# A hybrid attention / PEER layer on one core: two more ring slots for gathered rows, laid in the last eighth of the query weights

## The chip, the cores and the metric

One core of a Trainium2 chip runs the whole kernel. The metric is the device time of one execution in microseconds (us), as the median of several runs. TensorE is called PE, VectorE DVE, ScalarE ACT, GpSimd POOL and SyncE SP, as in the profile.

## What is computed

One layer over 1024 latent tokens of width 1024, with 256 context tokens. The token mixer is attention plus a bidirectional recurrence; its output goes through `w_out`, a norm and a residual. Then comes the part in which most of the time lies, product-key retrieval of single-neuron experts. The reference for it, per chunk of 128 tokens:

```python
q = (xc @ wq).reshape(PEER_CHUNK, PEER_HEADS, 2, PEER_DKEY // 2)
s = jnp.einsum('nhpd,hpkd->nhpk', q, subkeys).astype(jnp.float32)
s1, i1 = lax.top_k(s[:, :, 0], PEER_TOPK)
s2, i2 = lax.top_k(s[:, :, 1], PEER_TOPK)
...
top_s, pos = lax.top_k(cand_s, PEER_TOPK)
idx = jnp.take_along_axis(cand_i, pos, axis=-1)
g = jax.nn.softmax(top_s, axis=-1).astype(xc.dtype)
act = jax.nn.gelu(jnp.einsum('nhkd,nd->nhk', u[idx], xc))
return jnp.einsum('nhk,nhkd->nd', g * act, v[idx])
```

So each token picks 8 x 16 = 128 experts out of 16384, and for each of them a row of 1024 float32 of `u` and one of `v` are read.

## The kernel before

**Chunks.** The latent tokens are eight chunks of 128 (`NX = 8`). A chunk n passes through attention, a post part (output projection `out`, norms, the query projection `q(0)` to `q(3)` with `wq`, its transposes `turn_keyed`, the comparison with the subkeys `compare`), and a routing part on DVE that gives the indices of its 128 experts per token. Then its u rows and v rows are gathered. The work on the experts of chunk n runs beside the attention and post of chunk n+1.

**Gathers.** A "slot" is one indirect DMA of POOL (L619, in `gather`): one row of u or v for each of the 128 tokens, 4 KB to each of 128 partitions, 512 KB in all. A chunk has 128 u slots and 128 v slots, the kernel 2048 gathers. A u slot is consumed on DVE (L1565, `u_slots`), a product with `hx_cur` summed over the row. A v slot is consumed on PE (L2100, `v_slots`): two matmuls of 512 columns (four records in the profile) with a column of weights that ACT makes (L960, `SELS = 8` of them ahead).

**The ring.** Gathers land in `RING = 11` buffers of 4 KB a partition. The order of the gathers is fixed by a number for each, its place (`u_place`, `v_place`), and place p uses buffer p modulo 11. The order: chunk 0's 128 u slots; then per chunk 60 v slots (`LEAD`), which stand alone, then sixteen runs of twelve, 8 u slots of the next chunk and 4 v slots of this one, then 4 v slots (`TAIL`). The last chunk ends with its 68 v slots alone. Before a gather, `freed` lets POOL wait until the user of the place 11 back has counted up `u_used` (DVE) or `v_used` (PE). The user waits in `landed` for the buffer's own semaphore `got[r]`.

**PE's order** is written out by hand: `fill` puts v slots between the pieces of attention and post. In the post part of chunk n these are, in order: `out`, the transposes of the normed tokens, `q(0)`, `q(1)`, `q(2)`, `turn_keyed(0)`, `q(3)`, `compare(0)`, `turn_keyed(1)`, `compare(1)`. Each `q(i)` is eight matmuls over the slices kt = 0 to 7 of `wq`, 512 columns each (two records each in the profile, L2034). After routing, the indices are turned on PE (L2090) behind the lead's v slots, and DVE copies them out (L1589, in `turn_indices`); only then may the next chunk's v gathers start. DVE's L1401 is the maximum over the attention scores.

**SP's queue** is in program order: per chunk it loads `lc` (the recurrence's output, `load_l`, L495), the next `qz` (`load_qz`, L500), stores the finished chunk (L517) and loads a piece of x (`load_x`, L511). `wq` is loaded once, in two pieces; its last slice, `wq[:, KT - 1, :]`, is 8 KB a partition (L489).

**Memory.** A buffer `arena` holds most things. At its end lie `pr`, `pT`, `qc`, `lc` and `att`, the buffers of attention; `lc` and `att` (512 floats each) are dead from the end of the output projection of a chunk until the next `lc` is loaded.

## Time and profile before

| | |
|---|---|
| runs | 3435.26, 3441.04, 3443.61 us |
| median | 3441.04 us |
| span of the profiled execution (its only time) | 3447.3 us |
| mean granted clock of PE, share of full | 0.782 |
| busy PE / DVE / POOL / ACT | 2466.8 / 2047.0 / 2087.7 / 785.3 us |
| DMA | 1163.76 MB, mean 338 GB/s, of it 1084.36 MB from POOL's queue |
| gathers on POOL | 2048, 960.0 + 977.6 us busy |

The span runs from the first to the last instruction. Busy time counts neither waits nor the issue of DMAs by SP. "Idle before, released by" tells what event ended an engine's wait; where the name is "remote", the profile could not tie it to an instruction. The first eighth or so of the span is start-up and the recurrence; from 374 us on gathers run without end. One chunk takes some 372 us.

### The profile page before, as it was taken

What the parts mean: (1) busy time and instruction counts of PE and PEld (TensorE: products, weight loads), DVE (VectorE), ACT (ScalarE), POOL (GpSimd) and SP (SyncE); (2) the same over time, 40 slices, a digit from 0 to 9 for tenths busy, and PEclk for the clock granted to TensorE, in tenths of its full rate; (3) what the DMA queues carried; (4) which work ended last, traced back from release to release, by engine and by line L of the source; (5) the groups of instructions that cost most, each with busy time, mean ns of one, the idle gap of its engine ahead of it and who ended that gap; (6) DMA issues with size and microseconds to landing.
All of it is one profiled execution on the core that took longest, in us unless ns stands there. A gap on an engine that the chain in (4) does not pass through costs nothing.

```text
span 3447.3 us, 29321 instructions
## 1 busy us (share of the span) xinstructions
PE 2466.8 (72%) x9222; PEld 1078.6 (31%) x9222; DVE 2047.0 (59%) x4621; ACT 785.3 (23%) x1888; POOL 2087.7 (61%) x2167
## 2 busy tenths in 40 slices
PE   7978977768676776677777867787767766533476
PEld 4844654324221432134222422143213422000011
DVE  4785786666655666656656566665665666565300
ACT  2265111122112221222122221222122212100121
POOL 6910254566666666666666666666666666666665
PEclk8989987886789667865797578956796688855699
DMA  8533499799999999999999999999999999999998
GB/s 319 179 140 113 142 337 358 288 358 362 349 371 367 360 364 367 362 368 358 364 367 375 361 364 372 372 358 366 364 361 370 361 355 359 372 379 368 364 367 323
DMA packets 335937, 1163.76 MB, mean 338 GB/s; under 512 B 40485, under 2 KB 51365, under 8 KB 333608
## 3 DMA queue, kind: packets, MB, share of 16 engines
q0 software_dynamic: 297792, 1084.36, 83.6%
q1 hardware_dynamic: 37994, 77.54, 6.3%
q8 instruction: 76, 1.25, 0.1%
q14 instruction: 75, 0.61, 0.0%
HBM read 1148.13 MB, written 13.63 MB: 337 GB/s over the span
## 4 chain that ended last, share of the span: by engine, by line
PE 29%; POOL 16%; issue 14%; another core or an unknown queue 13%; DMA 12%; DVE 11%; ACT 4%; SPq 1%; DVEq 0%; ACTq 0%; POOLq 0%
POOL arena L619 16%; DMA arena<-in_v,arena 9%; PE psum L2100 9%; DVE arena L1565 6%; PE psum L1931 4%; PE psum L1899 4%; DMA arena<-in_u,idx_u 2%; PE psum L2034 2%; PE psum L1920 2%; PE psum L1946 2%; PE psum L1781 1%; PE psum L1956 1%; PE psum L1980 1%; ACT arena L883 1%
## 5 line engine op out<-in xcount | busy, mean ns | idle before, releaser
L1565 DVE CUSTOM_DVE_ANT_0 arena<-arena,psum 128x1024 f32<-128x1024 f32 x1024 | 1215.6, 1218 | 413.3 <-DMA arena<-in_u,idx_u 379.4
L619 POOL DMA_INDIRECT arena<-in_u,idx_u x1024 | 960.0, 937 | 652.8 <-issue 267.8
L2100 PE MATMUL psum<-arena 128*32 128x512 f32 x4096 | 1013.0, 744 | 445.6 <-DMA arena<-in_v,arena 305.4
L619 POOL DMA_INDIRECT arena<-in_v,arena x1024 | 977.6, 955 | 522.1 <-issue 256.8
L2100 PEld LDWEIGHTS psum<-arena 128*32 128x32 f32 x4096 | 181.8, 124 | 1185.3 <-issue 1036.6
L960 ACT ACTIVATE arena<-arena 128x32 f32<-128x32 f32 x1024 | 277.6, 314 | 1166.4 <-PE psum L2100 580.1
L1899 PE MATMUL psum<-kT,arena 64*128 64x512 f32 (+1 forms) x384 | 252.4, 810 | 56.2 <-issue 26.9
L1920 PE MATMUL psum<-ident,arena 128*128 128x128 f32 x560 | 137.5, 378 | 174.5 <-issue 110.3
L1401 DVE TENSOR_REDUCE small<-psum 128x1 f32<-128x1280 f32 x64 | 95.4, 1491 | 278.4 <-remote 220.8
L1931 PE MATMUL psum<-v,arena 128*128 128x64 f32 x1120 | 230.4, 395 | 27.3 <-ACT arena L883 24.0
L2034 PE MATMUL psum<-wbig,arena 128*128 128x512 f32 x512 | 242.4, 628 | 4.5 <-issue 3.4
L1931 PEld LDWEIGHTS psum<-v,arena 128*128 128x128 f32 x1120 | 221.4, 304 | 45.4 <-ACT arena L883 38.5
L883 ACT ACTIVATE arena<-psum 128x512 f32<-128x512 f32 x168 | 87.9, 523 | 403.6 <-remote 287.1
L1920 PEld LDWEIGHTS psum<-ident,arena 128*128 128x128 f32 x560 | 82.7, 186 | 296.6 <-issue 196.6
L1899 PEld LDWEIGHTS psum<-kT,arena 64*128 64x128 f32 x384 | 100.7, 279 | 185.7 <-issue 147.7
L2034 PEld LDWEIGHTS psum<-wbig,arena 128*128 128x128 f32 x512 | 100.7, 202 | 142.1 <-issue 140.3
L1426 DVE TENSOR_SCALAR small<-small 128x1 f32<-128x1 f32 x24 | 3.6, 152 | 225.8 <-ACT arena L977 164.4
L1964 PE MATMUL psum<-rows,ident 1*128 1x512 f32 x128 | 60.2, 824 | 77.9 <-issue 42.7
L1980 PE MATMUL psum<-arena 128*128 128x512 f32 x224 | 115.0, 668 | 0.0
L826 ACT ACTIVATE arena<-psum,small 128x64 f32<-128x64 f32 x64 | 20.0, 313 | 309.0 <-remote 197.5
L819 ACT ACTIVATE arena<-psum,small 128x1280 f32<-128x1280 f32 x64 | 84.8, 1325 | 23.6 <-issue 13.2
L1565 DVE DVE_READ_ACCUMULATOR2_ANT arena<- 128x1 f32 x1024 | 84.6, 83 | 0.0
(268 smaller groups left out, 2154.9 us busy)
## 6 DMA issues: line engine op xcount, KB each, us to landing
arena<-in_u,idx_u POOLq DMA_INDIRECT x1024
arena<-in_v,arena POOLq DMA_INDIRECT x1024
arena<-in_w_mod POOLq DMA_DIRECT2D x20, 512.0 KB, 4.3
wbig<-in_wq SPq DMA_DIRECT2D x1, 7168.0 KB, 19.7
arena<-in_w_mod SPq DMA_DIRECT2D x12, 512.0 KB, 4.1
arena<-in_xin SPq DMA_DIRECT2D x5, 1024.0 KB, 9.6
arena<-in_w_mod SPq DMA_DIRECT2D x2, 2048.0 KB, 10.7
wbig<-in_w_mod SPq DMA_DIRECT2D x2, 2048.0 KB, 20.5
```

The costliest lines, as they stand in the source:

```text
L619: pool.indirect_dma_start(ring[:, r, :], None, t[table], bass.IndirectOffsetOnAxis(idx[:, j:j + 1], 0)).then_inc(got[r], 16)
L819: A(pr, psum[:, score_at(n):score_at(n) + KEYS], ACT.Exp, scale=HD ** -0.5, bias=small[:, a:a + 1], accum_out=small[:, b:b + 1]).then_inc( ...
L883: A(pT[:, 4 * g:4 * g + k, :], bank(3)[:, 0:k * P], ACT.Copy).then_inc(S["pt_out"], 1)
L960: A(sel[:, j % SELS, :], hot[:, QP - 1 - i:2 * QP - 1 - i], ACT.Copy, scale=wT[:, n:n + 1])\
L1401: ch.link(V.tensor_reduce(small[:, a:a + 1], psum[:, score_at(n):score_at(n) + KEYS], AX, ALU.max))
L1565: V.tensor_tensor_reduce(ring[:, r, :], ring[:, r, :], hx_cur, 1.0, 0.0, ALU.mult, ALU.add, act_[:, j:j + 1]).then_inc(S["u_used"], 1)
L1899: ins = M(psum[:, at_ + b:at_ + b + w], lhsT=qc[o:o + 64, h // 2, :], rhs=kT[o:o + 64, b:b + w], start=True, stop=True)
L1920: ins = T(bank(3)[:, j * P:(j + 1) * P], pr[:, kt * P:(kt + 1) * P], ident[:, :])
L1931: ins = M(pv, lhsT=pT[:, kt, :], rhs=v[:, kt, 64 * (h % 2):64 * (h % 2) + 64], start=(kt == 0), stop=(kt == NTOK - 1))
L1980: return M(bank(i), lhsT=att[:, kt, :] if kt < 4 else lc[:, kt - 4, :], rhs=wo[:, kt, 512 * i:512 * i + 512], start=(kt == 4), stop=(kt == 3))
L2034: ins = M(bank(i), lhsT=hxT[:, kt, :], rhs=wq[:, kt, 512 * i:512 * i + 512], start=(kt == 0), stop=(kt == KT - 1))
L2100: ins = M(bank(4 + b)[QP * g:QP * g + QP, :], lhsT=sel[:, j % SELS, :], rhs=ring[:, r, 512 * b:512 * b + 512], start=(i == 0), stop=(i == ...
```

## The change

The ring gets 13 buffers. Eleven lie where they lay. Two lie over the last slice of the query weights, `wq[:, 7, 0:1024]` and `wq[:, 7, 1024:2048]`; `tile(r)` picks the place. Chunk 0 still uses that slice as it is, and POOL waits for `q_ready` 4 before the first gather into it. For chunks 1 to 7 the slice is loaded anew, in two halves of 512 KB, into the 1024 floats of `lc` and `att` (`wq_last`). The first half goes out when the output projection is done (`out_half`), and PE waits for it at the last slice of q(0); q(0) and q(1) use it. The second goes out when q(0) and q(1) are done (`q_ready` 4n+2), and PE waits for it at the last slice of q(2). The load of `lc` for the next chunk now waits until all four q are done. In `freed` and `landed` nothing is edited, but with `RING` 13 every wait names the user of 13 places back. To make room for semaphores some of the start-up are merged (`hot_made` into `filled`, `tanh_c` and `lam_exp`, `modT_ready` and `mod_rows`); this changes no order. Line numbers move: L619 is L637, L1565 is L1585, L2034 is L2059, L2100 is L2124, L2042 is L2066, L495 is L501, L500 is L515, L511 is L526, L517 is L532, L1589 is L1609.

```diff
@@ -54,7 +54,7 @@
 PAIRS = FULL + (TOPK - WIDE) * NARROW
 SLOTS = PH * TOPK
 HALF_SLOTS = SLOTS // 2
-RING = 11
+RING, ARENA_SLOTS = 13, 11
 QUADS, QP = 4, 32
 SELS = 8
 LABEL = 2 * NK
...
@@ -223,10 +223,12 @@
         qc = view(4 * P, 4, P)
         lc = view(4 * P, 4, P)
         att = view(4 * P, 4, P)
+        LC_AT = ATT_AT + 2 * KEYS + 4 * P
+        wq_last = arena[:, LC_AT:LC_AT + D]
 
         at[0] = 0
         wo = view(KT * D, KT, D)
-        ring = view(RING * D, RING, D)
+        ring = view(ARENA_SLOTS * D, ARENA_SLOTS, D)
         xm_new, xm_next, xm_cur = (view(D) for _ in range(3))
         qz = view(QZ_ROW)
         hx_new = qz[:, 0:D]
...
@@ -322,6 +324,10 @@
 
             return (c * STRIDE + place) % RING
 
+        def tile(r):
+
+            return ring[:, r, :] if r < ARENA_SLOTS else wq[:, KT - 1, (r - ARENA_SLOTS) * D:(r - ARENA_SLOTS + 1) * D]
+
         h_scr = nc.dram_tensor("h_scr", (NX, P, KT * P), F32, kind="Internal").ap()
         qz_scr = nc.dram_tensor("qz_scr", (NX, P, QZ_ROW), F32, kind="Internal").ap()
         l_scr = nc.dram_tensor("l_scr", (LF, P, SEQ), F32, kind="Internal").ap()
...
@@ -491,8 +497,17 @@
 
             def load_l(n):
 
-                sp.wait_ge(S["out_half"], 2 * n)
+                wait(sp, "q_ready" if n > 1 else "out_half", 4 * n if n > 1 else 2)
                 sp.dma_start(lc, l_scr[:, :, n * P:n * P + P].rearrange("f p c -> p f c")).then_inc(S["l_loaded"], 16)
+
+            def load_wq_last(n):
+
+                for half in range(2):
+                    if half:
+                        sp.wait_ge(S["q_ready"], 4 * n + 2)
+                    else:
+                        sp.wait_ge(S["out_half"], 2 * n + 2)
+                    sp.dma_start(wq_last, wqv[:, KT - 1, D * half:D * half + D]).then_inc(S["wq_last_loaded"], 16)
 
             def load_qz(n):
 
...
@@ -549,14 +564,17 @@
             sp.wait_ge(S["q_half_stored"], 16 * (NX - 2))
             sp.wait_ge(S["z_half_stored"], 16 * (NX - 2))
             load_x(1)
+            load_wq_last(1)
             load_l(2)
             load_qz(2)
             load_x(2)
             for k in range(NX - 3):
+                load_wq_last(k + 2)
                 load_l(k + 3)
                 load_qz(k + 3)
                 store(k)
                 load_x(k + 3)
+            load_wq_last(NX - 1)
             for c in range(NX - 3, NX):
                 store(c)
             sp.wait_ge(S["out_stored"], 16 * NX)
...
@@ -613,10 +631,10 @@
             for i in range(2):
                 pool.wait_ge(S["lru_stored%d" % i], 16 * LF // 2)
             ch.link(nc.gpsimd.memset(hot, 0.0))
-            nc.gpsimd.memset(hot[:, QP - 1:QP], 1.0).then_inc(S["hot_made"], 1)
+            nc.gpsimd.memset(hot[:, QP - 1:QP], 1.0).then_inc(S["filled"], 1)
 
             def gather(table, idx, j, r):
-                pool.indirect_dma_start(ring[:, r, :], None, t[table],
+                pool.indirect_dma_start(tile(r), None, t[table],
                                         bass.IndirectOffsetOnAxis(idx[:, j:j + 1], 0)).then_inc(got[r], 16)
 
             def u_gather(c, j):
...
@@ -624,6 +642,8 @@
                 if j % HALF_SLOTS == 0:
                     pool.wait_ge(S["idx_ready"], 2 * c + j // HALF_SLOTS + 1)
                     pool.sem_inc(S["passed"], 1)
+                if c == 0 and j == ARENA_SLOTS:
+                    pool.wait_ge(S["q_ready"], 4)
                 freed(c, u_place(c, j))
                 gather("u", idx_u, j, slot(c, u_place(c, j)))
 
...
@@ -1562,7 +1582,7 @@
 
                 for j in range(lo, hi):
                     r = landed(dve, c, u_place(c, j))
-                    V.tensor_tensor_reduce(ring[:, r, :], ring[:, r, :], hx_cur, 1.0, 0.0, ALU.mult, ALU.add,
+                    V.tensor_tensor_reduce(tile(r), tile(r), hx_cur, 1.0, 0.0, ALU.mult, ALU.add,
                                            act_[:, j:j + 1]).then_inc(S["u_used"], 1)
 
             def weights(c):
...
@@ -2031,8 +2051,12 @@
                             turn_first(i - 1)
                         if n == 0 and i and kt == 4:
                             compare_first(i - 1)
-                        ins = M(bank(i), lhsT=hxT[:, kt, :], rhs=wq[:, kt, 512 * i:512 * i + 512],
-                                start=(kt == 0), stop=(kt == KT - 1))
+                        w = wq[:, kt, 512 * i:512 * i + 512]
+                        if n and kt == KT - 1:
+                            if i % 2 == 0:
+                                pe.wait_ge(S["wq_last_loaded"], 16 * (2 * n - 1 + i // 2))
+                            w = wq_last[:, 512 * (i % 2):512 * (i % 2) + 512]
+                        ins = M(bank(i), lhsT=hxT[:, kt, :], rhs=w, start=(kt == 0), stop=(kt == KT - 1))
                     ins.then_inc(S["q_ready"], 1)
 
                 def turn_keyed(u):
...
@@ -2098,7 +2122,7 @@
                     for b in range(2):
                         g = (q + 2 * b) % QUADS
                         ins = M(bank(4 + b)[QP * g:QP * g + QP, :], lhsT=sel[:, j % SELS, :],
-                                rhs=ring[:, r, 512 * b:512 * b + 512], start=(i == 0), stop=(i == QP - 1))
+                                rhs=tile(r)[:, 512 * b:512 * b + 512], start=(i == 0), stop=(i == QP - 1))
                     ins.then_inc(S["v_used"], 1)
 
             def none(b):
```

SP's queue in the loop over the chunks; `in_wq` is the weights' tensor, `arena` the place of `wq_last`, `lc`, `qz` and x. Before:

```order
87 L495 DMA arena<-l_scr 128x4x128 [waits out_half]
88 L500 DMA arena<-qz_scr 128x1152 [waits hx_moved]
89 L511 DMA arena<-in_xin 128x1024 [waits xm_moved]
90 L495 DMA arena<-l_scr 128x4x128 [waits out_half]
91 L500 DMA arena<-qz_scr 128x1152 [waits hx_moved]
92 L517 DMA out<-arena 128x1024 [waits out_ready]
```

Now:

```order
87 L510 DMA arena<-in_wq 128x1024 [waits out_half]
88 L510 DMA arena<-in_wq 128x1024 [waits q_ready]
89 L501 DMA arena<-l_scr 128x4x128 [waits q_ready]
90 L515 DMA arena<-qz_scr 128x1152 [waits hx_moved]
91 L526 DMA arena<-in_xin 128x1024 [waits xm_moved]
92 L510 DMA arena<-in_wq 128x1024 [waits out_half]
93 L510 DMA arena<-in_wq 128x1024 [waits q_ready]
94 L501 DMA arena<-l_scr 128x4x128 [waits q_ready]
95 L515 DMA arena<-qz_scr 128x1152 [waits hx_moved]
```

Two loads stand ahead of the load of `lc` in each chunk, which waits for `q_ready` in place of `out_half`.

PE in the post part of a chunk, from the first matmul of q(0) to `turn_keyed(0)`; the rows left out are v slots. Before:

```order
1211 L2034 MATMUL psum<-wbig,arena 128x512 [waits wq_loaded,hxT_out]
1212 L2034 MATMUL psum<-wbig,arena 128x512 x10
...
1221 L2034 MATMUL psum<-wbig,arena 128x512 x11
...
1230 L2034 MATMUL psum<-wbig,arena 128x512 x2
1231 L2042 MATMUL psum<-ident,arena 128x128 [waits q_out]
1232 L2042 MATMUL psum<-ident,arena 128x128 x7
```

Now (`psum<-arena` on L2059 is a matmul with `wq_last`):

```order
1223 L2059 MATMUL psum<-wbig,arena 128x512 [waits wq_loaded,hxT_out]
1224 L2059 MATMUL psum<-wbig,arena 128x512 x6
1225 L2059 MATMUL psum<-arena 128x512 [waits wq_last_loaded]
1226 L2059 MATMUL psum<-wbig,arena 128x512 x3
...
1235 L2059 MATMUL psum<-wbig,arena 128x512 x4
1236 L2059 MATMUL psum<-arena 128x512
1237 L2059 MATMUL psum<-wbig,arena 128x512 x6
...
1246 L2059 MATMUL psum<-wbig,arena 128x512
1247 L2059 MATMUL psum<-arena 128x512 [waits wq_last_loaded]
1248 L2066 MATMUL psum<-ident,arena 128x128 [waits q_out]
1249 L2066 MATMUL psum<-ident,arena 128x128 x7
```

The order of matmuls is as before. The eighth matmul of each q reads `arena`, and the one of q(0) and of q(2) waits for a load.

## Rows read from the trace of the kernel before

**Rows 1.** The page: busy time (share) of the engines; the DMA in 40 slices.

```profile
PE 2466.8 (72%) x9222; PEld 1078.6 (31%) x9222; DVE 2047.0 (59%) x4621; ACT 785.3 (23%) x1888; POOL 2087.7 (61%) x2167
...
DMA  8533499799999999999999999999999999999998
```

**Rows 2.** Waits of POOL, whole kernel: total us, times, longest.

```profile
POOL arena L619 <- PE psum L2100: 259.6, 171, 20.1
POOL arena L619 <- remote: 187.2, 82, 4.9
POOL arena L619 <- DVE arena L1565: 148.5, 116, 23.1
```

**Rows 3.** Stretches: an attention, a lead, without a stall, after one, last v slots.

```profile
core 0: us, PE busy (x) PEld busy (x) DVE busy (x) ACT busy (x) POOL busy (x), PEclk, DMA share, GB/s
1119.00:1236.00 117.00, 93.15 (x340) 49.83 (x340) 73.62 (x130) 25.93 (x64) 75.62 (x81) 0.62 0.97 361
1384.00:1490.00 106.00, 73.15 (x296) 17.24 (x295) 61.23 (x258) 28.87 (x85) 68.49 (x72) 0.90 0.98 373
3010.00:3034.00 24.00, 5.99 (x18) 0.87 (x16) 17.99 (x29) 1.28 (x4) 16.27 (x18) 0.63 1.02 418
3036.00:3046.00 10.00, 6.80 (x16) 0.65 (x12) 1.46 (x3) 1.61 (x5) 7.50 (x8) 0.50 0.78 258
3262.00:3434.00 172.00, 129.81 (x500) 23.06 (x492) 3.52 (x5) 36.13 (x124) 110.54 (x117) 0.97 0.97 364
```

**Rows 4.** Timeline of PE and POOL, 3020 to 3037 (idle before, released by).

```profile
3020.83 5.67 PE L2100 MATMUL psum<-arena 128*32 128x512 f32 x16 [10.50 <-DMA arena<-in_v,arena]
...
3029.28 0.94 POOL L619 DMA_INDIRECT arena<-in_v,arena  x1 [0.30 <-issue]
...
3035.80 2.30 PE L2100 MATMUL psum<-arena 128*32 128x512 f32 x6 [9.31 <-DMA arena<-in_v,arena]
...
3036.26 0.94 POOL L619 DMA_INDIRECT arena<-in_v,arena  x1 [4.80 <-remote]
```

**Rows 5.** Waits of DVE in the attention 1119 to 1236.

```profile
DVE small L1401 <- remote: 40.2, 6, 8.1
```

**Rows 6.** Line 1589 (turned indices copied, DVE): its waits, us and times.

```profile
  remote: 58.6, 4
  PE psum L2090: 12.4, 3
```

**Rows 7.** Waits of POOL in 1384:1490, in 2990:3262, in 3262:3434.

```profile
POOL arena L619 <- PE psum L2100: 17.3, 14, 2.6
...
POOL arena L619 <- remote: 32.4, 9, 4.8
...
POOL arena L619 <- PE psum L2100: 33.8, 34, 3.6
```

**Rows 8.** Waits of POOL in the post 1236 to 1384.

```profile
POOL arena L619 <- remote: 21.2, 7, 4.9
```

**Rows 9.** DMA view of 1090 to 1110: SP's queue, packets, MB, share.

```profile
q1 hardware_dynamic: 288, 1.05, 14.0%
```

**Rows 10.** Timeline of SP, PE and DVE in a post and the lead behind it.

```profile
1287.33 0.37 SPq L495 DMA_DIRECT2D arena<-l_scr  x1
...
1318.58 9.71 PE L2034 MATMUL psum<-wbig,arena 128*128 128x512 f32 x22
...
1339.78 11.13 PE L2034 MATMUL psum<-wbig,arena 128*128 128x512 f32 x21 [1.09 <-issue]
...
1352.69 1.98 PE L2034 MATMUL psum<-wbig,arena 128*128 128x512 f32 x4
...
1473.25 0.69 DVE L1289 SCALAR_TENSOR_TENSOR arena<-arena 128x512 f32<-128x512 f32 x1
```

**Rows 11.** The page: DMA issues, KB each, us to landing.

```profile
arena<-in_w_mod SPq DMA_DIRECT2D x12, 512.0 KB, 4.1
...
wbig<-in_wq SPq DMA_DIRECT2D x1, 1024.0 KB, 8.2
```

More of the change, by code:

```diff
@@ L331, in layer @@
             "gains_loaded", "wm_loaded0", "wm_loaded1", "wm_loaded2", "wm_loaded3", "wm_used",
-            "acc_loaded", "staged_in0", "staged_in1", "mod_summed", "mod_rows", "mod_out",
-            "silu_ready", "tanh_c", "g1_ready", "a2_ready", "b2_ready", "g2_ready",
-            "modT_ready", "kvl_loaded", "x_loaded", "x_sq",
+            "acc_loaded", "staged_in0", "staged_in1", "mod_summed", "mod_turned", "mod_out",
+            "silu_ready", "c_tanh_lam_exp", "g1_ready", "a2_ready", "b2_ready", "g2_ready",
+            "kvl_loaded", "x_loaded", "x_sq",
             "x_var", "x_sd", "xn_ready", "xT_first", "xT_ready", "hT_vec", "hT_act", "kv_ready", "lru_ready",
@@ L691, in _ @@
             act.wait_ge(S["c_loaded"], 48)
-            A(csil, ccol, ACT.Tanh, scale=0.5).then_inc(S["tanh_c"], 1)
+            A(csil, ccol, ACT.Tanh, scale=0.5).then_inc(S["c_tanh_lam_exp"], 1)
             def x_norm(m):
@@ L801, in _ @@
             act.wait_ge(S["lam_ready"], 1)
-            A(lt[:, 1, :], lt[:, 0, :], ACT.Exp, scale=-1.0).then_inc(S["lam_exp"], 1)
+            A(lt[:, 1, :], lt[:, 0, :], ACT.Exp, scale=-1.0).then_inc(S["c_tanh_lam_exp"], 1)
             for m in range(1, NTOK // 2 - 1):
@@ L1085, in _ @@
             post(1, none)
-            act.wait_ge(S["hot_made"], 1)
+            act.wait_ge(S["filled"], 7)
             gelu(0)
@@ L1117, in _ @@
             V = nc.vector
-            dve.wait_ge(S["tanh_c"], 1)
+            dve.wait_ge(S["c_tanh_lam_exp"], 1)
             dve.wait_ge(S["filled"], 2)
@@ L1311, in _ @@
             V.tensor_copy(rowm, bank(4)).then_inc(S["mod_cols"], 1)
-            dve.wait_ge(S["modT_ready"], 1)
+            dve.wait_ge(S["mod_turned"], 1)
             dve.wait_ge(S["acc_loaded"], 32)
@@ L1615, in _ @@
             negmax(0, 0)
-            dve.wait_ge(S["mod_rows"], 1)
+            dve.wait_ge(S["mod_turned"], 2)
             dve.wait_ge(S["gains_loaded"], 48)
@@ L1729, in mod_sum @@
                                 start=True, stop=True)
-                ins.then_inc(S["mod_rows"], 1)
+                ins.then_inc(S["mod_turned"], 1)
             def keys(m, tt):
@@ L1835, in _ @@
                 ins = T(bank(6)[:, j * P:(j + 1) * P], rowm[:, j * P:(j + 1) * P], ident[:, :])
-            ins.then_inc(S["modT_ready"], 1)
+            ins.then_inc(S["mod_turned"], 1)
             pe.wait_ge(S["kvl_loaded"], 16)
```

8 lines of the change are left out of this document (4 added, 4 removed).

## Prediction

> **What bounds the kernel now.** I read the page first. Over the whole span no engine is full: PE is busy 72%, POOL 61%, DVE 59%, while the DMA line is at nine tenths or more from the ninth slice on [rows 1]. The loop is 2048 gathers. One takes 0.94 us of POOL and 0.30 of "issue" ahead of the next [rows 4], so back to back one leaves every 1.24 us, and 2048 of them are 2540 us of the span. What makes it longer stands in POOL's waits: 259.6 us for PE's v slots, 187.2 "remote", 148.5 for DVE's u slots [rows 2]. These are waits for a ring slot, and the change is aimed at them.
>
> Whether POOL or the memory sets the pace is told by the table of stretches [rows 3]. In an attention and in a lead the DMA engines show a share of 0.97 and 0.98 at 361 and 373 GB/s. But from 3010 to 3034, when POOL issues without a stall, they move 418 GB/s at 1.02, and just after a stall 258 at 0.78. The share hardly tells these states apart, the rate does: 418 GB/s is a gather of 0.524 MB each 1.25 us, POOL's own pace. So I hold the gathers to be limited by POOL and its stalls, not by the memory.
>
> How a stall arises is seen late in the kernel [rows 4]. POOL issues a v gather at 3029.28 and one more, then waits 4.80 us until 3036.26. The slot that it needs is that of eleven places before, whose matmuls by the records lie in the block 3020.83 + 5.67 = 3026.50. It is let go only when PE begins its next slots at 3035.80, and these wait for the gather of 3029.28 to land, 6.5 us after its issue. So the loop is: issue, landing, PE's next start, report, 7.0 us in all, and eleven slots let POOL issue two gathers in it. The Trainium skill (TensorE: Matmul & The Clock Gate, Part 3) has matmuls ending strictly in order, so that one increment on the last one is sound, and counts tens of ns for increments; here the report stands over 9 us behind the modelled end. By the page's figure there would be no stall to win here, and 11 us of the sum below would go.
>
> **The change, part by part.**
>
> *Two slots more.* The need of each gather moves two gathers back, 2 x 1.24 = 2.48 us. The stall of 4.80 becomes 2.3; one of up to 2.5 goes. What that is worth differs by stage.
>
> Attention: 81 gathers in 117 us, 1.44 each. DVE waits 40.2 us there for scores [rows 5], and PE, busy 93 of 117 at a clock of 0.62 [rows 3], sets the pace; POOL's stalls are its slack. I take **0** for the attention of every chunk.
>
> Lead: DVE has its routing done and then waits for the turned indices (L1589), which stand behind the 60 v slots on PE: 58.6 + 12.4 = 71.0 us in seven chunks, 10.1 each [rows 6]. POOL stalls for slots there 17.3 us, at most 2.6 at a time [rows 7], so two more slots could take nearly all. The bounds are 0 and -71, since behind that DVE's own routing is next. PE's late reports and the landings stay, so I take half: **-35**.
>
> Post: seven stalls, 21.2 us, the longest 4.9 [rows 8]. At most 7 x 2.48 = 17.4 goes. The stalls follow on each other, and where one is shortened POOL sooner stands before the next, as PE's q and turns take as long as before; I take -7, in the six chunks that have both tables in flight: **-42**, bounds 0 and -104.
>
> Part without attention (2990 to 3262): nine stalls, 32.4 us, longest 4.8 [rows 7]. At most 9 x 2.48 = 22. For the same reason half: **-11**.
>
> Last v slots (3262 to 3434): 33.8 us in 34 stalls [rows 7], 117 gathers in 172 us, where 117 x 1.24 = 145 [rows 3]. Bounds 0 and -27; PE is busy 130 of the 172 there and its slots follow each landing, so a quarter of the stalls: **-9**.
>
> *Fourteen loads of 512 KB.* Each chunk but the first loads 1.05 MB more, the bytes of two gathers. The nearest row is the stretch 1090 to 1110, where a store and a load of together 1.05 MB took 14.0% of 20 us: 2.8 us of all the engines [rows 9]. If POOL's pace and not the memory is the limit, some of it hides; I count all, 7 x 2.8 = **+20**. Bounds 0 and 20.
>
> *PE's new waits.* The first half is released by what now releases `lc`, at 1287.33, and q(0) reaches its last slice at 1318.58 + 14/22 x 9.71 = 1324.8 [rows 10]: 37 us for a load. The second half is released by q(1). Of the block at 1339.78 nine of 21 records belong to q(1): it ends at 1344.6. q(2) needs the half at its last matmul, at 1352.69 + 0.99 = 1353.7 [rows 10]. That is 9.1 us. Loads of 512 KB took 4.1 us on SP, one of 1024 KB took 8.2 [rows 11]; amid gathers I expect 6 to 8. Bounds 0 and, if q(1)'s report came 9.5 us late as in rows 4, 8.2 + 9.5 - 9.1 = 8.6. Between q(1)'s end and the need PE runs nearly without a break, unlike in rows 4, so I take 1 us in each chunk: **+7**. Behind that wait stand q(2)'s turns, q(3) and v slots on PE; ACT's and DVE's copies of q would be late, and the comparison.
>
> *Moved and merged.* SP's load of `lc` now stands behind both loads and behind q(3), so is issued some 75 us later than 1287.33. DVE reads it at 1473.25 [rows 10]: 256 KB have over 100 us. The load of `qz` behind it waits for DVE's copy anyway. POOL's new wait for `q_ready` 4 at the twelfth gather of chunk 0 is met before that chunk has indices. The merged semaphores belong to the start-up and keep its order. All at 0, covered by these times; if `lc` came late, DVE's mixing and the next `out` would be.
>
> **Sum.** -35 - 42 - 11 - 9 + 20 + 7 = -70. The profiled execution has a span of 3447.3, which is 6.3 above the median 3441.04. 3447.3 - 70 = 3377, less 6.3: **3371 us**, chance 0.50. A measurement can tell 0.3% (10 us) from no change.
>
> **Rivals.** (1) The memory is the limit, not POOL. For it: a share of 0.97 in every stage, with gaps in POOL's issue too short to empty the queues. Against it: 418 GB/s in rows 3. Then a slot more only makes gathers queue longer, and the loads' 7.34 MB are paid in full: at 361 GB/s 20 us, 3441 + 20 = **3461**, slower. It decides wherever the transfers in flight already keep the engines fed. Chance 0.17. The Trainium skill (DMA: Bandwidth & Descriptors, Specifications) gives a limit of about 358 GB/s of HBM for a core. By that rule the loop is at its ceiling and this rival is the outcome, with 7.34 MB / 358 GB/s = 20.5 us; the 418 GB/s kept up for 24 us speak against it.
> (2) q(1)'s report is late, and PE waits 8.6 us in seven chunks where I took 1: 3371 + 53 = **3424**, hardly faster; with a post that gains half as much, 3445. For it rows 4, against it that PE doesn't pause at that place. Chance 0.12.
> (3) The slots don't do what they say: PE reports only when it begins its next slots, so the stalls gather again two places later, and what is left pays for the loads: **3441**. Chance 0.08.
> (4) Every bound is reached: -71 - 104 - 22 - 27 + 20 = -204, or **3237**; half way from my sum to it, 3304. For it: POOL's stalls are 595 us in all [rows 2]. Chance 0.13.
>
> **Range.** 3300 to 3464: it leaves out the far half of (4) and what runs worse than (1). Faster by over 0.3%: 0.50 + 0.13 + 0.03 of (2) = 0.66. Slower: (1) and 0.01 of other mishaps = 0.18. The same: the rest, 0.16.
>
> **What would show it.** Right: in the part without attention the stalls of 4.8 us are about 2.3; the wait at L1589 (now L1609) falls to a half; a post is some 3 us shorter and an attention still 117; PE waits under 2 us at the last slice of q(2). Wrong: fewer stalls of POOL with the same GB/s and longer landings (rival 1), or several us on the `in_wq` loads (rival 2).

## The result, and the profile after

The changed kernel takes 3465.11 us in the median of 12 runs (3451.24 to 3478.39), the kernel before beside it 3442.19 (12 runs, 3431.53 to 3453.91). The ratio is 1.0065, with a 95% interval of 1.0046 to 1.0084: slower by 23 us, where 3371 was forecast. It lies one microsecond above the range. The profiled execution has a span of 3462.5 us, 15.2 above that of before.

The page of the changed kernel, with the rows that answer to [rows 1]:

```profile
PE 2409.3 (70%) x9222; PEld 1080.9 (31%) x9222; DVE 2039.2 (59%) x4621; ACT 784.2 (23%) x1888; POOL 2084.6 (60%) x2167
...
DMA  8533499699999999999999999999999998999998
```

At this level nothing seems to have happened: POOL is as busy, the DMA line as full. POOL's waits, to be held against [rows 2] (the waits for a slot in `wbig` are listed apart):

```profile
POOL arena L637 <- PE psum L2124: 227.8, 120, 11.3
POOL arena L637 <- remote: 169.7, 74, 5.6
...
POOL arena L637 <- DVE arena L1585: 109.4, 80, 24.6
...
POOL wbig L637 <- PE psum L2124: 46.9, 17, 26.9
POOL wbig L637 <- remote: 27.9, 11, 4.7
...
POOL wbig L637 <- DVE arena L1585: 15.1, 13, 6.2
```

Waiting for slots took 259.6 + 187.2 + 148.5 = 595.3 us before. Now it is 506.9 for the eleven in the arena and 89.9 for the two in `wbig`, together 596.8. Two more slots took nothing off the stalls, nor off the mean "remote" one: 187.2 / 82 = 2.28 us before, 197.6 / 85 = 2.32 after.

The same stages, columns as in [rows 3] and to be held against them: an attention, the lead and the post in front of it (of chunk 3), and the part without attention.

```profile
1501.00:1617.00 116.00, 94.30 (x333) 51.78 (x336) 73.91 (x129) 25.82 (x64) 76.40 (x83) 0.59 0.98 366
1396.00:1501.00 105.00, 73.26 (x288) 16.79 (x280) 60.73 (x257) 29.36 (x85) 71.41 (x73) 0.83 0.99 377
1243.00:1396.00 153.00, 106.77 (x370) 46.25 (x366) 95.20 (x161) 26.39 (x65) 96.70 (x104) 0.77 0.94 364
3016.00:3280.00 264.00, 82.45 (x256) 13.45 (x256) 144.61 (x239) 18.02 (x58) 174.81 (x188) 0.63 0.96 376
```

The attention takes 116 us where it took 117, the lead 105 where it took 106, the post 153 where it took 148. This post is the one that grew most: by the records the posts of chunks 2 to 7 take 152.4 us on average where they took 150.0. A gather takes 264 / 188 = 1.404 us in the part without attention. The kernel before had 272 / 192 = 1.417 in the stretch for which [rows 7] give the stalls:

```profile
2990.00:3262.00 272.00, 101.27 (x279) 15.06 (x278) 148.82 (x245) 23.73 (x73) 179.84 (x192) 0.59 0.95 371
```

The stall that was to shrink from 4.80 us [rows 4] to 2.3 is still there. POOL's timeline in the same part:

```profile
3034.03 0.94 POOL L637 DMA_INDIRECT arena<-in_v,arena  x1 [0.31 <-issue]
3039.92 0.93 POOL L637 DMA_INDIRECT arena<-in_u,idx_u  x1 [4.95 <-PE psum L2124]
...
3073.17 0.93 POOL L637 DMA_INDIRECT arena<-in_u,idx_u  x1 [3.73 <-remote]
...
3106.31 0.93 POOL L637 DMA_INDIRECT arena<-in_v,arena  x1 [4.88 <-remote]
```

The kernel before had here

```profile
3070.42 0.94 POOL L619 DMA_INDIRECT arena<-in_v,arena  x1 [4.64 <-remote]
```

which is 34.2 us behind 3036.26; now two intervals of 33.2 us stand there, with stalls of 3.73 to 4.95 us at their ends. POOL starts again 5.89 us after its last issue (3034.03 to 3039.92). In [rows 4] this was 0.94 + 4.80 = 5.74 us. This stall hasn't shrunk, it has moved back with POOL's last gather: in [rows 4] POOL stopped before the third of four v gathers, now it stops two places later, before the u gather behind them.

The copy of the turned indices on DVE shows what the stages add up to. Its first and last start after:

```profile
L1609 DVE CAST arena<-psum x8: 284/291/292, 427.3 to 2996.6; 128x128 uint32<-128x128 f32 x8
...
  remote: 37.9, 3
  issue: 20.5, 3
  PE psum L2114: 3.9, 1
```

and before:

```profile
L1589 DVE CAST arena<-psum x8: 285/292/292, 423.2 to 2972.1; 128x128 uint32<-128x128 f32 x8
```

Between the first copy and the last lie 2569.3 us after and 2548.9 before, so the seven chunks cost 20.4 us more; the start cost 4.1, and from the last copy to the end it is 465.9 in place of 475.2 us, 9.3 less. 20.4 + 4.1 - 9.3 = 15.2, the whole difference of the spans. The copy waits 62.3 us in all, where it was 71.0 [rows 6].

The largest change among the waits is in a place that the prediction named only as a risk. In the post part ACT copies the transposed queries after `turn_keyed(0)` (L934 before, L954 after), and PE's `compare(0)` waits for it. What ACT waited for at this line, before:

```profile
  remote: 6.8, 2
```

and after:

```profile
  remote: 108.3, 6
```

That is six chunks, and 18.1 us of waiting in each. One of them in the timeline of the changed kernel (PE, ACT, PE):

```profile
1363.84 1.04 PE L2066 MATMUL psum<-ident,arena 128*128 128x128 f32 x8
...
1382.35 1.02 ACT L954 ACTIVATE arena<-psum 128x1024 f32<-128x1024 f32 x1 [12.39 <-remote]
...
1383.43 3.79 PE L2074 MATMUL psum<-skT,arena 128*128 128x128 f32 x16 [11.69 <-issue]
```

The transposes end at 1364.88 by their record; ACT gets to know it at 1382.35, 17.5 us later, and the comparison starts at 1383.43. In the kernel before it was 1355.55 and 1360.70, 5.2 us, with columns to make for ACT in between:

```profile
1354.51 1.04 PE L2042 MATMUL psum<-ident,arena 128*128 128x128 f32 x8
...
1360.70 1.00 ACT L934 ACTIVATE arena<-psum 128x1024 f32<-128x1024 f32 x1
```
In these places "remote" marks a report that comes late. It doesn't prove one by itself, for the trace of this kernel, and of the one before, lacks many records of reports: of DVE's 1024 for the u slots the kernel before has 416. That ACT starts so late is measured all the same.

### The profile page after: what moved, and what is told of

It reads as the page before. It is cut to its first block, busy times and chain, and to the rows that moved or that the text cites. A ratio compares the mean times of both kernels' runs of the same rounds, so it can differ in the third digit from the quotient of the medians.

```text
span 3462.5 us, 29335 instructions
## 1 busy us (share of the span) xinstructions
PE 2409.3 (70%) x9222; PEld 1080.9 (31%) x9222; DVE 2039.2 (59%) x4621; ACT 784.2 (23%) x1888; POOL 2084.6 (60%) x2167
## 4 chain that ended last, share of the span: by engine, by line
PE 31%; another core or an unknown queue 18%; issue 15%; POOL 14%; DMA 10%; ACT 6%; DVE 5%; SPq 0%; DVEq 0%; ACTq 0%; POOLq 0%
POOL arena L637 12%; PE psum L2124 9%; DMA arena<-in_v,arena 6%; PE psum L1951 4%; PE psum L1919 3%; PE psum L2059 3%; POOL wbig L637 2%; DVE arena L1585 2%; PE psum L1940 2%; PE psum L1966 2%; PE psum L1976 1%; PE psum L1801 1%; ACT arena L903 1%; DMA wbig<-in_v,arena 1%
## 5 line engine op out<-in xcount | busy, mean ns | idle before, releaser
L1585 DVE CUSTOM_DVE_ANT_0 arena<-arena,psum 128x1024 f32<-128x1024 f32 x866 | 1028.8, 1217 | 318.3 <-DMA arena<-in_u,idx_u 233.4
L637 POOL DMA_INDIRECT arena<-in_v,arena x868 | 824.4, 950 | 587.5 <-issue 215.7
L2124 PE MATMUL psum<-arena 128*32 128x512 f32 x3472 | 836.6, 762 | 354.4 <-DMA arena<-in_v,arena 217.9
L637 POOL DMA_INDIRECT arena<-in_u,idx_u x866 | 814.8, 941 | 432.6 <-issue 241.0
L2124 PEld LDWEIGHTS psum<-arena 128*32 128x32 f32 x3472 | 155.9, 126 | 925.1 <-issue 811.8
L2059 PE MATMUL psum<-wbig,arena 128*128 128x512 f32 x456 | 223.6, 633 | 23.3 <-issue 22.2
L1585 DVE CUSTOM_DVE_ANT_0 wbig<-wbig,psum 128x1024 f32<-128x1024 f32 x158 | 189.7, 1217 | 55.5 <-DMA wbig<-in_u,idx_u 52.8
L2124 PE MATMUL psum<-wbig,arena 128*32 128x512 f32 x624 | 174.8, 744 | 62.2 <-DMA wbig<-in_v,arena 43.1
L637 POOL DMA_INDIRECT wbig<-in_v,arena x156 | 148.9, 955 | 114.3 <-PE psum L2124 46.9
L637 POOL DMA_INDIRECT wbig<-in_u,idx_u x158 | 148.1, 938 | 59.4 <-issue 44.2
L2059 PEld LDWEIGHTS psum<-wbig,arena 128*128 128x128 f32 x456 | 89.8, 203 | 142.9 <-issue 141.2
```

Of the source, the lines that this page charges most:

```text
L637: pool.indirect_dma_start(tile(r), None, t[table], bass.IndirectOffsetOnAxis(idx[:, j:j + 1], 0)).then_inc(got[r], 16)
L1585: V.tensor_tensor_reduce(tile(r), tile(r), hx_cur, 1.0, 0.0, ALU.mult, ALU.add, act_[:, j:j + 1]).then_inc(S["u_used"], 1)
L2059: ins = M(bank(i), lhsT=hxT[:, kt, :], rhs=w, start=(kt == 0), stop=(kt == KT - 1))
L2124: ins = M(bank(4 + b)[QP * g:QP * g + QP, :], lhsT=sel[:, j % SELS, :], rhs=tile(r)[:, 512 * b:512 * b + 512], start=(i == 0), stop=(i == ...
```

## The experiments

Eighteen runs in five series, each beside the kernel before. In three of the series the kernel before took 3443, 3443 and 3463 us, in two 3083 us, and one chip was in series of both kinds, so it isn't the chip; what sets it I don't know. Since the ratios differ between the two kinds, each result names the kernel before beside it. The theories: **A**, the memory sets the average rate. **B**, the forecast: each slot is worth 1.24 us of each stall. **C**: PE's semaphore reports are held while the DMA engines run full, at 420 GB/s, and more slots only make such bursts longer. **D**, put up after `g512` had ruled out C in this form: they are held while POOL issues gathers without a gap, whatever the bytes, and come 4 to 5.5 us after its last issue. **E**: the reports are late for some other reason.

### Loads alone, slots alone, fewer slots

`r11_loads` is the changed kernel with `RING` 11, `r13_noloads` has 13 slots without the fourteen loads and PE's waits for them, `r9` the kernel before with nine.

```diff
-RING, ARENA_SLOTS = 13, 11
+RING, ARENA_SLOTS = 11, 11
```

> The changed kernel with eleven ring slots: the fourteen loads, their waits and the moved load of lc stand alone. Theory A (the gathers' average rate is fixed by the memory; the ring is worth nothing, the loads are paid in full): 3442 + 20 = 3462 us, as the changed kernel. Theory B (slots are worth what was forecast, -97 us, and the loads and their waits cost far more than forecast): 3442 + 120 = about 3560. Theory C (PE's reports are held while the DMA engines run at 420 GB/s; longer bursts through more slots make them later, and that is the loss): the loads cost at most 10, 3442 to 3452.

Measured: 3446.86 us beside 3443.0, ratio 1.003 (1.0006 to 1.0054). The loads cost 4 us by the medians and 10 by the ratio, as C said, and far from B.

```diff
-                    sp.dma_start(wq_last, wqv[:, KT - 1, D * half:D * half + D]).then_inc(S["wq_last_loaded"], 16)
...
-                            if i % 2 == 0:
-                                pe.wait_ge(S["wq_last_loaded"], 16 * (2 * n - 1 + i // 2))
```

> Thirteen slots, but the fourteen loads and PE's waits for them are left out, so the last slice of the query projection of chunks 1 to 7 is computed with what lies in the arena. Theory A: 3442, no change from before. Theory B: -97 from 3442, about 3345. Theory C: 3445 to 3460, slower than before though nothing is loaded, with compare(0) late again.

Measured: 3457.98 us, ratio 1.005 (1.0026 to 1.0075). The slots alone lose 15 us, though nothing more is loaded; the last slice of q is then computed with what lies in the arena. What ACT waited for at the copy of the transposed queries, with 13 slots and no loads:

```profile
  remote: 93.9, 5
```

and with 11 slots and all loads:

```profile
  remote: 4.7, 1
```

Between these two the late report goes with the slots and not with the loads; `g512` below will show it with eleven slots too. A and B are both out: A because loads and slots don't behave as it says (it had 3462 and 3442), B by more than 100 us.

```diff
-RING = 11
+RING = 9
...
-        ring = view(RING * D, RING, D)
+        ring = view(11 * D, 11, D)
```

> The kernel before with nine slots in place of eleven, nothing else. Theory A: 3442, within 10. Theory B (each stall grows by 2.48 us, as it was to shrink): about +97, 3540. Theory C: bursts are shorter, reports are less late; between 3430 and 3470, far from +97.

Measured: 3440.77 us, ratio 1.0011 (0.9979 to 1.0042). Two slots fewer cost nothing that can be measured. C's range held as well; of the three theories B alone (3540) is excluded by this run. Again in the fifth series, beside 3462.91:

> Nine slots, beside a series in which reports may be prompt (kernel before near 3083). Then seven slots were 1.0271, thirteen without loads 0.9985. If the worth of a slot falls off steadily, nine are 1.003 to 1.010. With held reports (before near 3442): 1.001, as the first time.

Measured: 3471.33 us, ratio 1.0012 (0.9989 to 1.0035), the same.

### Are the bytes the cause?

`g512` moves half a row with each gather.

```diff
-                pool.indirect_dma_start(ring[:, r, :], None, t[table],
+                pool.indirect_dma_start(ring[:, r, 0:512], None, t[table].rearrange("n (a b) -> (n a) b", a=2),
...
-                    V.tensor_tensor_reduce(ring[:, r, :], ring[:, r, :], hx_cur, 1.0, 0.0, ALU.mult, ALU.add,
+                    V.tensor_tensor_reduce(ring[:, r, :], rows[:, :], hx_cur, 1.0, 0.0, ALU.mult, ALU.add,
```

> The kernel before with gathers of half the bytes: 2 KB to a partition (half a row, from the first half of the table). DVE's operation keeps its 1024 elements but multiplies a constant tile with hx and writes the slot; PE multiplies the whole slot. Eleven slots, every wait and the count of gathers stay. At POOL's pace of 1.24 us the DMA engines then move some 211 GB/s and not 418. Theory A and C (the memory or its full queues stand behind the stalls and behind PE's late reports): PE's reports come within 1 or 2 us of their ends, POOL's stalls for v slots fall by more than a half, and the time falls to 3050 to 3250, where PE or POOL is the bound. Theory B (the loop of ring, engines and reports has nothing to do with the bytes): the stalls and the time stay, 3400 to 3450.

Measured: 3452.39 us beside 3442.59, ratio 1.0024 (0.9998 to 1.005). Half the bytes, and no time won. The stretch from 1200 to 2700 of this kernel (columns as in [rows 3]):

```profile
1200.00:2700.00 1500.00, 1047.53 (x3883) 440.98 (x3883) 909.25 (x2177) 327.80 (x855) 975.47 (x1017) 0.75 0.63 183
```

and of the kernel before:

```profile
1200.00:2700.00 1500.00, 1104.42 (x3936) 456.38 (x3933) 928.22 (x2195) 330.63 (x866) 975.15 (x1029) 0.75 0.97 365
```

That is 1017 gathers against 1029 in 1500 us, at 183 against 365 GB/s. It ends theory A and every account in bytes, and C too as it stood: both had 3050 to 3250, and B alone had the time stay. The reports are as late. POOL and ACT in this kernel:

```profile
1333.94 0.95 POOL L619 DMA_INDIRECT arena<-in_u,idx_u  x1 [0.30 <-issue]
1339.33 0.95 POOL L619 DMA_INDIRECT arena<-in_u,idx_u  x1 [4.45 <-remote]
...
1338.99 0.60 ACT L927 ACTIVATE arena<-psum 128x512 f32<-128x512 f32 x1 [22.15 <-remote]
```

and in the kernel before:

```profile
1334.38 0.94 POOL L619 DMA_INDIRECT arena<-in_u,idx_u  x1 [0.30 <-issue]
1340.24 0.94 POOL L619 DMA_INDIRECT arena<-in_u,idx_u  x1 [4.93 <-remote]
...
1339.90 0.60 ACT L927 ACTIVATE arena<-psum 128x512 f32<-128x512 f32 x1 [18.77 <-remote]
```

In both POOL stops, and ACT gets PE's report of q(0) 5.05 us (1333.94 to 1338.99) and 5.52 us (1334.38 to 1339.90) after POOL's last gather was issued, having waited 22.15 and 18.77 us. In these two places the report comes when POOL has been silent for some 5 us, whatever the size of the gathers.

PE doesn't run on undisturbed meanwhile. The row below and that of 1339.78 in [rows 10] both lie inside q(1) of the kernel before, whose matmuls have nothing to wait for there, and between the two PE stands idle for 1.09 us:

```profile
1337.68 1.01 PE L2034 MATMUL psum<-wbig,arena 128*128 128x512 f32 x1 [0.82 <-issue]
```

PE, ACT and POOL go on within half a microsecond (1339.78, 1339.90, 1340.24). So it may not be the report alone that is held. Such idle times of PE ahead of instructions that wait for nothing sum up to 28 us in the kernel before, 32 in the changed one, 39 in `g512`, and to nothing where reports are prompt.

The copy of the transposed queries in `g512`, which has eleven slots:

```profile
  remote: 99.4, 6
```

So late reports there don't need thirteen slots. What the two kernels share is where POOL's run of gathers ends. By the records, in `g512` all six reports came at the end of a run of 24 gathers, 5.0 to 5.1 us after its last, and in the changed kernel five of six did, 5.2 us after it (the one shown above, at 1382.35, came 2.5 us after the gather of 1379.81). In the kernel before, four of six came 4 us after the last of a run of 14, 3.7 to 4.9 us late; but one came 9.8 us late and 0.75 us after a gather, so silence of POOL isn't always what brings them.

Nor is the price of the late copy clear. The comparison of the six chunks starts on average at 142.8 us of the post in `g512`, and at 137.6 in `r9`, where it was 131.0 before; yet `r9` took no longer, and `g512` some 10 us, with an interval that still includes no change.

### Fewer gathers in flight, a slower POOL

`r11_cap5` and `r11_cap4` let POOL wait until the gather five or four places back has landed; `r11_pace1` and `r11_pace1x2` put one or two small memsets ahead of each gather.

```diff
+            def landed_before(c, place):
+
+                place += c * STRIDE - CAP
+                if place >= 0:
+                    pool.wait_ge(got[place % RING], 16 * (place // RING + 1))
```

> The kernel before; POOL waits besides until the gather five places back has landed, so at most five are in flight and no backlog builds up in the DMA queues. Theory A: slower, since the memory is given less to do: 3460 to 3550. Theory B: slower too, since POOL waits more: over 3460. Theory C: PE's reports come within 2 us of their ends instead of up to 17, POOL's waits for PE fall by a half, and the time is the same or better: 3400 to 3445.

Measured: 3472.19 us beside 3443.0, ratio 1.0097 (1.0066 to 1.0129). C had said the same or better, with reports within 2 us: wrong on both. One of POOL's waits:

```profile
POOL arena L620 <- remote: 132.7, 85, 3.9
```

Nor does this fit D: by the records POOL's longest run without a gap fell from 25 gathers to 15, and runs of ten and more from 113 to 15, yet of the 1024 reports for v slots only 411 came within 0.3 us of the end of their record, where it was 304.

> The kernel before, POOL waits until the gather four places back has landed (five places back cost 0.97%). Theory C in its strong form (only a full queue holds the reports): lateness of reports falls under 2 us; the rate of the transfers falls too, 3450 to 3560. Theory A: slower by more than with five, 3500 to 3700.

Measured: 3805.49 us beside 3442.59, ratio 1.1073 (1.103 to 1.1117), slower than C had said. But its profile says more than its time. POOL's waits:

```profile
POOL arena L620 <- DMA arena<-in_u,idx_u: 395.6, 349, 4.3
POOL arena L620 <- DMA arena<-in_v,arena: 366.2, 322, 3.2
...
POOL arena L620 <- PE psum L2109: 41.0, 46, 10.2
```

With four in flight POOL hardly waits for PE any more, 41.0 us where it was 259.6 + 187.2, and no wait of POOL is "remote". Now 919 of the 1024 reports are prompt; POOL pays for that with 762 us of waits for landings. Whether it is POOL's pauses (no run is longer than five) or the number of gathers in flight that makes them prompt, the two runs don't tell apart.

```diff
+                for _ in range(1):
+                    pool.wait_ge(S["pool_chain"], ch.k - 3)
+                    at4 = 1 * (ch.k % 4)
+                    ch.step(nc.gpsimd.memset(idle[:, at4:at4 + 1], 0.0))
```

> The kernel before with one small memset of POOL ahead of each gather, so that a gather leaves about every 1.34 to 1.40 us in place of 1.24 and the DMA engines stay below 418 GB/s in bursts. Theory C (PE's reports are held while the engines of the DMA run full): fewer and shorter holds, POOL's long stalls shrink by what the pace costs, 3400 to 3445. Theory A: 3442 within 10, since the average is 1.45 us a gather anyway. Theory B: each gather costs 0.1 more wherever POOL sets the pace, 3500 or over.

Measured: 3486.93 us, ratio 1.0141 (1.0099 to 1.0183).

> As before it with two memsets, about 1.45 us a gather or a little over. Theory C: holds nearly gone, but no burst makes up for a stall: 3440 to 3520. Theory A: as much. Theory B: 3600.

Measured: 3534.34 us, ratio 1.0282 (1.0242 to 1.0322). Neither tells anything of a slower pace, because the pace did not change: the median interval of gathers stayed at 1.24 us, the memsets went into the 0.30 us between them. That they cost 44 and 92 us all the same is not explained.

### Cutting POOL's run ahead of the transposes

If a run of gathers holds the report of `turn_keyed(0)`, then a pause of POOL at this place must bring it.

```diff
             def v_gather(c, j):
...
+                if j == 116 and c + 2 < NX:
+                    pool.wait_ge(S["qT_ready"], 2 * (c + 2) + 3)
                 freed(c, v_place(c, j))
```

> The changed kernel; POOL waits besides, in the post of chunks 2 to 7, ahead of the v gather 116 of the older chunk until PE has reported the end of turn_keyed(0). In the changed kernel that report came 17.5 to 20.7 us after the modelled end of the transposes, in the kernel before 2.8 to 9.8, and compare(0) started at 141 us of the stage in place of 131. Theory D (PE's reports are held while POOL issues gathers without a gap and come some 4 to 5.5 us after its last issue, whatever the bytes; more slots only make the run longer): the report comes within 7 us, compare(0) starts near 131, the post falls from 152.4 to about 150, the kernel to 3440 to 3455. Theory E (the reports are late for another reason, such as the loads or where the slots lie): report and compare(0) as late as before the pause, and the pause comes on top, 3465 to 3500.

> The kernel before with the same pause. Theory D: there the report is 3 to 10 us late already, so little is won: 3430 to 3445. Theory E: 3445 to 3480.

Measured in the third series, where the kernel before took 3082.6 us: 3092.52 us for 13 slots, ratio 1.0033 (1.0021 to 1.0045), and 3082.62 for 11, ratio 0.9999 (0.999 to 1.0008). Nothing was late there, so there was nothing to cut. The same again in the fourth and the fifth series:

> The pause in the changed kernel again, beside the changed kernel. The first time PE's reports were prompt in every run of the series (0.0 us late, the kernel before at 3082.6 us) and the pause had nothing to cut. If reports are held in this series (kernel before near 3442): Theory D 3440 to 3455 with compare(0) near 131, theory E 3465 to 3500. If they are prompt (before near 3083): as then, ratio 1.003.

> The pause in the changed kernel once more. With held reports: theory D 3440 to 3455 and compare(0) near 131, theory E 3465 to 3500. With prompt reports: 1.003, as twice before, and the question stays open.

Measured: 3094.75 beside 3082.57, ratio 1.0036 (1.0023 to 1.0048), again without late reports; and then 3472.62 beside 3462.91, ratio 1.0026 (1.0003 to 1.0049), with them. In the last the pause did at this place what theory D says. ACT's waits at the copy of the transposed queries are now, for nine of fourteen, with no "remote" left:

```profile
  PE psum L2068: 25.9, 9
```

and the pair of PE and ACT that was 17.5 us apart:

```profile
1373.83 1.04 PE L2068 MATMUL psum<-ident,arena 128*128 128x128 f32 x8
...
1374.90 1.02 ACT L956 ACTIVATE arena<-psum 128x1024 f32<-128x1024 f32 x1 [3.46 <-PE psum L2068]
```

The comparison of the six chunks starts on average at 128.8 us of the post, where it was 140.9 in the changed kernel and 131.0 before (worked out from the records of all six). The ratio falls from 1.0065 to 1.0026; the two intervals, 1.0046 to 1.0084 and 1.0003 to 1.0049, still touch, they are of two series, and the changed kernel had no run in the fifth. In microseconds 3472.62 lies in E's range (3465 to 3500) and not in D's, both given for a series in which the kernel before takes 3442; as a ratio it lies in D's. That the pause removes the late report at this place is shown, and E, by which it would have stayed, is out; that it wins time is not shown.

### Where reports are prompt

> The changed kernel again. With held reports 1.0065 of before, as in its first runs. With prompt reports theory D says that the 13 slots cost nothing and may win what the sum of stalls allows: POOL waits for PE only 112 us in all there, so 0 to -20 us for the slots, and the loads cost 4 to 10: ratio 0.997 to 1.003. If the loss does not come from held reports, 1.0065 as before.

> Thirteen slots without the fourteen loads. With held reports 1.005, as the first time. With prompt reports the slots alone: 0.994 to 1.000; over 1.003 would say that slots cost time without any late report.

> Eleven slots with the fourteen loads and their waits. With held reports 1.003, as the first time. With prompt reports the DMA engines are at 418 GB/s nearly throughout, so the loads are paid in full: up to +20 us, 1.003 to 1.0065.

The edits are none and the two of the first series. The kernel before took 3082.57 us beside them.

| kernel | us | ratio | 95% interval |
|---|---|---|---|
| 13 slots, loads (the changed kernel) | 3093.97 | 1.0033 | 1.0021 to 1.0044 |
| 13 slots, no loads | 3077.83 | 0.9985 | 0.9975 to 0.9995 |
| 11 slots, loads | 3098.66 | 1.0051 | 1.0034 to 1.0068 |

The parts add up: loads +16.1, slots -4.7, both 11.4 = 3093.97 - 3082.57. The stretch of the changed kernel from 1200 to 2700 there, and POOL's waits:

```profile
1200.00:2700.00 1500.00, 1159.50 (x4384) 414.66 (x4382) 1052.76 (x2534) 387.80 (x963) 1099.26 (x1163) 0.85 1.02 416
...
POOL arena L637 <- DVE arena L1585: 123.1, 177, 16.8
...
POOL arena L637 <- PE psum L2124: 109.6, 235, 4.1
...
POOL wbig L637 <- PE psum L2124: 40.0, 44, 20.7
```

416 GB/s on average, not in bursts, and not one wait of POOL is "remote". ACT's waits at the copy of the transposed queries, all fourteen:

```profile
  PE psum L2066: 32.1, 14
```

The kernel with 11 slots and the pause, as good as the kernel before there (ratio 0.9999), shows in the same stretch

```profile
1200.00:2700.00 1500.00, 1172.89 (x4398) 419.06 (x4398) 1060.82 (x2546) 388.50 (x967) 1112.08 (x1173) 0.85 1.02 415
```

which is 1173 gathers, where the kernel before had 1029 in it with late reports (the row under `g512`). The two kinds of series lie some 360 us apart, fifteen times what the change costs. Late reports, and PE standing idle with nothing to wait for, are what the traces show on one side alone; that they make up all of the 360 isn't shown.

Here the slots finally win, and little, since POOL stands for slots much less; and 7.34 MB at 416 GB/s are 17.6 us, of which 16.1 were measured. How long a u gather takes from issue to landing, with seven, eleven and thirteen slots (`r7`, `r11_pause`, `r13_again`), is the last number of each row:

```profile
arena<-in_u,idx_u POOLq DMA_INDIRECT x1024, 6.4
...
arena<-in_u,idx_u POOLq DMA_INDIRECT x1024, 9.7
...
arena<-in_u,idx_u POOLq DMA_INDIRECT x866, 12.5
```

A slot more mostly makes the gathers queue longer, and the loads are paid nearly in full. That is what rival (1) described, in the series where it was not asked.

> Gathers of 64 rows in place of 128, to partitions 0 to 63 alone; rows stay 4 KB, so half the bytes and half the descriptors (halving the bytes of each row changed nothing: 3452). DVE multiplies a constant tile with hx and writes the slot, as there. Theory D1 (what holds the reports is the handling of descriptors by POOL and the DMA queues): lateness falls, POOL's long stalls fall, 3050 to 3350. Theory D2 (what holds them is that POOL's instructions follow each other, whatever they move): as the kernel before, 3430 to 3460.

Measured (third series, prompt): 3071.88 us beside 3082.6, ratio 0.996 (0.9946 to 0.9975). `g64` gathers 64 rows in place of 128; DVE's line is changed as in `g512`.

```diff
-                pool.indirect_dma_start(ring[:, r, :], None, t[table],
-                                        bass.IndirectOffsetOnAxis(idx[:, j:j + 1], 0)).then_inc(got[r], 16)
+                pool.indirect_dma_start(ring[0:64, r, :], None, t[table],
+                                        bass.IndirectOffsetOnAxis(idx[0:64, j:j + 1], 0)).then_inc(got[r], 16)
```

No report was late anyway, so it can't tell D1 from D2. POOL's gathers leave every 1.20 us in place of 1.24. Nor does it show that bytes don't count where reports are prompt: from 1200 to 2700 the DMA engines move 211 GB/s, half as much, but at the same share of 1.02, and by the records a packet takes 315 ns where it took 159. What this run halves in bytes it doesn't halve in the DMA engines' time.

> The kernel before with seven slots. Nine were as fast as eleven. Theory B (2.48 us a stall and two slots) gave +97 for nine already and would give +190: 3630. Theory D (the length of a run only moves the hold): until the slots are fewer than a landing and a use take, 6.5 / 1.24 = 5 to 6, little changes: 3445 to 3520.

Measured (same series, `RING = 7` in the same way as nine): 3163.21 us beside 3082.6, ratio 1.0271 (1.0255 to 1.0286). So with prompt reports the slots from seven to eleven are worth 80 us, and the two above eleven 4.7. Nine slots were run only where reports are late.

## Why the prediction was wrong, step by step

**What bounds the kernel.** "Limited by POOL and its stalls, not by the memory" was right for these series: half the bytes took as long. Rival (1), which would have had the time right (3461), is wrong here as a mechanism, though near the truth in the series with prompt reports. With it falls what the Trainium skill's limit of about 358 GB/s (DMA: Bandwidth & Descriptors, Specifications) would make of this case: it gives the time within 4 us, but the core moved 416 GB/s over 1500 us in `r13_again`, and at 183 GB/s the kernel was no faster.

**The step that failed** is "the stall of 4.80 becomes 2.3". It read the loop of [rows 4] as issue, landing, PE's next start, report, 7.0 us from the issue of a v gather, so that two more slots would fill 2.48 of them. That takes the moment of release as given, so that slots only move the need. But the release moves with POOL's last issue: POOL starts again 5.74, 5.89, 5.86 and 5.39 us after it in four of the places shown (in [rows 4], after 3034.03, 1334.38 and, with half the bytes, 1333.94). POOL with two more slots stops two gathers later, and the release comes later with it. These are the long stalls, and they stay at 3.7 to 5 us; most others end sooner, by the mean of 2.3 us. In the sum the slots stood for -97 us in all; POOL's waits for slots went from 595.3 to 596.8, and the slots by themselves cost 15 us (`r13_noloads`). Why PE's reports come late at all stays open. The Trainium skill (TensorE: Matmul & The Clock Gate, Part 3) has tens of ns for a report; the series with prompt reports agree with it (as does the pair 1373.83 + 1.04 and 1374.90 with the pause), the others do not, by some 20 us at the most. I take it for chance that PE started again 0.46 us before the release in [rows 4]; in the post of the changed kernel the report of 1382.35 came while PE stood still until 1383.43.

**Lead**, forecast -35: the wait of L1609 fell by 8.7 us, from 71.0 to 62.3, and the lead shown by 1. With half the bound I had counted on a mechanism that wasn't there.

**Post**, forecast -42 for slots: it grew by 5 us in the chunk shown. The post shown is the largest case, the mean of the six is +2.4. POOL's run of gathers, moved by the slots, now ends behind the transposes, and the report of `turn_keyed(0)` came late: ACT's "remote" waits for it went from 6.8 us in two chunks to 108.3 in six. The late next thing after a stall was named (comparison, ACT's copies), but only behind the new load, not behind the slots.

**Part without attention and last v slots**, forecast -20: from the last copy of indices to the end 9.3 us were won. Right in sign.

**Loads**, forecast +20 for bytes: +4 to +10 where reports are late, +16.1 where they are prompt. The size was right for the case in which the DMA engines run at 416 GB/s. That part of it hides in POOL's stalls fits these numbers; no run shows it by itself.

**PE's new waits**, forecast +7:

```profile
650.43 2.07 PE L2059 MATMUL psum<-arena 128*128 128x512 f32 x2 [4.28 <-DMA arena<-in_wq]
```

This is PE's only wait for these loads, 4.28 us in chunk 1, where by the records q(1)'s report was 6.2 us late and with it the load: rival (2), once in seven chunks. In the other six the 1 us that was counted didn't come up.

**Chunk 1** was not looked at. Its post took 11 us longer (91.1 and 102.0, from DVE's last maximum to its copy of `hx`, by the records), half of the loss of the seven chunks. The posts of the other six cost 14.4 us together, and attention and lead win 5 back. The held report of q(1) and the load behind it are part of chunk 1's.

**Rivals.** (3), at 0.08, is nearest in what it says of the slots: the stalls gather again two places later. Its reason, that PE reports when it begins its next slots, isn't what the runs show: at 1382.35 PE reported while it stood still. Its time, 3441, left out what the slots themselves cost, 15 us in `r13_noloads`. I had the 9.8 us between record and report in hand, and wrote a theory of its release from one place. A second, ACT's copy of q(0) at 1339.90 with its "remote" wait of 18.77 us, would have shown before the run that other reports of PE are late too.

## What to carry to other kernels

When a wait ends "remote", look what the engine that should have released it had recorded, and when: a report that comes long after the record's end is a wait of another kind, and a buffer more won't shorten it. Before a deeper ring is paid for, run a shallower one: here two slots fewer cost nothing, and two more didn't pay. Look also at how long a gather takes to land as slots are added. Read the release of a stall in two places where different engines wait, before pricing it.

## What was not expected of the hardware

PE's semaphore reports came some 20 us after the modelled end at the most of the matmul while POOL issued indirect gathers back to back, and often in a burst some 5 us after POOL stopped; PE itself stood idle up to 2.2 us at a time with nothing to wait for. Half the bytes made no difference (183 GB/s, 22.15 us at ACT), four gathers in flight made them nearly prompt (919 of 1024), five did not (411). In two series of the same kernels there was no such delay at all, and the kernel before took 3083 us and not 3443 or 3463. What switches it, and by what path POOL's gathers hold PE's reports, stays open. The runs show that it isn't the bytes and, one chip having been in both kinds of series, not the chip alone.
